# Two norm boundaries of a decoder step: one scale moved behind the contraction, and a third output chunk in the first feed-forward pass

## The reference

```python
for l in range(DEPTH):                       # DEPTH = 2
    hp, hs = rms_norm(xp, norm_mix_pre[l]), rms_norm(xs, norm_mix_pre[l])
    ...                                      # layer 0: retention and gated MLP; layer 1: sparse attention
    xp = xp + rms_norm(mp, norm_mix_post[l])
    xs = xs + rms_norm(ms, norm_mix_post[l])
    fp, cp = conv_ffn(rms_norm(xp, norm_ffn_pre[l]), zeros, f_w_in[l], ...)
    ...
    xp = xp + rms_norm(fp, norm_ffn_post[l])
    xs = xs + rms_norm(fs, norm_ffn_post[l])
```

## Time and profile before

| | us |
|---|---|
| median of 3 runs | 1612.62 (1607.88 to 1613.97) |
| profiled execution, whole | 1613.73 |
| its span in the profile | 1612.0 |
| PE busy | 1567.7 |
| DVE busy | 836.5 |
| ACT busy | 690.7 |
| POOL busy | 229.9 |

### The profile page before, as it was taken

The page is one execution under the profiler, slowest core; times in us unless marked ns, Lnnn a source line. Parts: engine busy times, 40 slices in busy tenths (PEclk is TensorE's granted clock), DMA queues, the critical chain, the costliest instruction groups (busy, mean ns, idle before and its releaser), DMA issues.

```text
span 1612.0 us, 29956 instructions
## 1 busy us (share of the span) xinstructions
PE 1567.7 (97%) x12323; PEld 1401.0 (87%) x12323; DVE 836.5 (52%) x1359; ACT 690.7 (43%) x1311; POOL 229.9 (14%) x574
## 2 busy tenths in 40 slices
PE   8999999999999999998999999999989999999998
PEld 7799989699999999996677566667989999999997
DVE  4855452655532555568234676743585552355523
ACT  5222134555532545432323565655545552355522
POOL 3000001300000000002013444422020000000001
PEclk9999999999999999999999899999999999999999
DMA  7322337023233332322344400033203324233231
GB/s 229 101 81 81 100 80 188 17 83 101 62 95 96 86 97 62 95 70 80 114 132 92 150 9 2 1 119 78 79 27 92 90 60 116 79 96 87 63 86 56
DMA packets 180274, 138.38 MB, mean 86 GB/s; under 512 B 11408, under 2 KB 164272, under 8 KB 180112
## 3 DMA queue, kind: packets, MB, share of 16 engines
q1 hardware_dynamic: 172288, 113.26, 24.4%
q0 software_dynamic: 7888, 23.79, 5.1%
HBM read 128.21 MB, written 13.01 MB: 88 GB/s over the span
## 4 chain that ended last, share of the span: by engine, by line
PE 89%; DVE 6%; ACT 2%; issue 1%; POOL 1%; DMA 0%; POOLq 0%; ACTq 0%; DVEq 0%
PE gemm L1150 42%; PE gemm L714 18%; PE gemm L725 9%; PE misc L683 6%; PE gemm L1290 3%; PE misc L1321 2%; PE misc L888 1%; DVE hL L1909 1%; PE misc L1426 1%; PE gemm L888 1%; PE misc L761 1%; DVE y L1983 1%; DVE y L1969 1%; PE misc L844 1%; PE misc L1315 0%
## 5 line engine op out<-in xcount | busy, mean ns | idle before, releaser
L1898 DVE TENSOR_TENSOR wL<-raw,wH 128x2048 fp32r<-128x2048 f32 (+1 forms) x106 | 219.6, 2072 | 151.0 <-ACT wH L1460 150.8
L1150 PE MATMUL gemm<-hH,wH 128*128 128x272 f32 x1280 | 268.5, 291 | 0.2
L1150 PE MATMUL gemm<-hH,wL 128*128 128x272 f32 x1280 | 264.8, 288 | 0.0
L1150 PE MATMUL gemm<-hL,wH 128*128 128x272 f32 x1280 | 264.0, 288 | 0.0
L1460 ACT ACTIVATE wH<-raw 128x2048 fp32r<-128x2048 f32 (+2 forms) x110 | 185.9, 1690 | 74.0 <-PE gemm L725 37.5
L1150 PEld LDWEIGHTS gemm<-hH,wH 128*128 128x128 f32 x1280 | 200.6, 188 | 6.1 <-issue 4.1
L1150 PEld LDWEIGHTS gemm<-hL,wH 128*128 128x128 f32 x1280 | 201.1, 188 | 0.0
L1150 PEld LDWEIGHTS gemm<-hH,wL 128*128 128x128 f32 x1280 | 199.9, 189 | 0.0
L2262 DVE SCALAR_TENSOR_TENSOR conv<-up,rows_t,conv 128x560 f32<-128x560 f32 x88 | 70.6, 802 | 208.2 <-ACT conv L1460 208.2
L1460 ACT ACTIVATE up<-gemm 128x32 f32<-128x32 f32 (+2 forms) x264 | 66.0, 324 | 175.0 <-PE gemm L1150 153.7
L714 PE MATMUL gemm<-hH,wH 128*128 128x272 f32 (+1 forms) x624 | 132.6, 294 | 0.9 <-issue 0.6
(11 more groups left out here) (416 smaller groups left out, 2725.5 us busy)
## 6 DMA issues: line engine op xcount, KB each, us to landing
raw<-in_f_w_in SPq DMA_DIRECT2D x88, 512.0 KB, 4.9
raw<-in_f_w_out SPq DMA_DIRECT2D x32, 704.0 KB, 4.6
raw<-in_e_w_in SPq DMA_DIRECT2D x12, 1024.0 KB, 5.1
raw<-in_o_w_in SPq DMA_DIRECT2D x10, 1024.0 KB, 5.1
raw<-in_e_w_out SPq DMA_DIRECT2D x4, 1024.0 KB, 6.1
raw<-in_o_w_out SPq DMA_DIRECT2D x16, 256.0 KB, 6.7
pages<-in_cache_cmp POOLq DMA_DIRECT2D x10, 256.0 KB, 4.1
xin<-in_x_prompt SPq DMA_DIRECT2D x4, 512.0 KB, 6.5
```

The costliest lines, as they stand in the source:

```text
L1150: ins = pe.matmul(gemm[odd][:, n, 0:TH], w, x[:, k, n * TH:(n + 1) * TH], start=(k == 0 and part == 0), stop=(k == nk - 1 and part == 2))
L1898: order(dve.tensor_tensor(unit_view(wL, u), unit_view(raw, u), unit_view(wH, u).bitcast(F32), ALU.subtract), lo_ready)
```

## The change

Six edits, four at place A and behind it, three at place B (POOL's is common to both).

1. Place A (`plain_norm`, `fill_plain`): h is x times the gain only; norm 4's scale is left out of it. For each tile DVE scales y straight from RS, adds x + y at once, and makes `hL` by one operation out of x, the gain and `hH`; ACT makes `hH` with the gain as its scale. The total stands behind tile 1, its root on ACT behind `hH` of tile 2, and the split of O_IN+1 with the reciprocal behind tile 4.
2. Norm 4's scale is spread by PE inside O_IN+1, ahead of the last tile's products, kept as a row by ACT, turned into a column of tokens by PE (`turn_rstd`), and kept again by ACT (`keep_rstd`). The copies out of PSUM of all token units then multiply by it; the sample rows get one more DVE operation a unit; the gates' sigmoid moves behind their turn, in five operations. The split of O_IN+2 stands ahead of this on ACT, and ahead of the sample rows on DVE.
3. POOL adds no tile at norms 3 and 5 (`POOLED_POSTS` keeps it at the first and last norm); DVE adds all eight.
4. Place B (`expanded_norms`): scaling y, adding, scaling x of one tile follow each other on DVE, the second and third waiting for the one ahead; `hL` is one tile behind. The split of F1+1 stands behind tile 2's step.
5. `first_three` in place of `first_pair`: from tile 3 on, PE also makes c2, the first chunk of F1+1, in banks b4 and b7; tiles 0 to 3 of it are made at tile 3, then one at each tile.
6. Units F1+1 and F1+2 are written out ahead of the loop (`peeled`), since F1+1 has only c3 left; idle products: 16 behind A's spread; 8 and 16 behind B's two spreads (before 10 and 10 at each place).

```diff
+            def third_products(k):
+                at = k * 256
+                wh, wl = wH[:, (F1 + 1) % 2, at:at + P], wL[:, (F1 + 1) % 2, at:at + P]
+                for part, (w, x) in enumerate(((wh, hH), (wh, hL), (wl, hH))):
+                    for z in range(2):
+                        ins = pe.matmul(misc[:, 3 * z, 0:TH], w, x[:, k, z * TH:(z + 1) * TH],
+                                        start=(k == 0 and part == 0), stop=(k == DC - 1 and part == 2))
+                return ins
-            def first_pair(u, fill):
+            def first_three(u, fill):
...
                         if k == DC - 1:
                             order(ins, gemm_done)
+                    if k == 3:
+                        unit(u + 1)
+                        for earlier in range(3):
+                            third_products(earlier)
+                    if k >= 3:
+                        ins = third_products(k)
+                order(ins, gemm_done)
...
+            def turn_rstd():
+                pe.wait_ge(squared, EXPANDED[3].spread_kept())
+                for t in range(NT):
+                    w = NS if t == 0 else P
+                    ins = pe.matmul(b7[0:w, t:t + 1], rstd_row[0:1, tile_start(t):tile_start(t) + w], ident[0:1, 0:1], start=True, stop=True)
+                order(ins, summed)
...
                 if u == O_IN + 1:
                     for k in ks:
                         pe.wait_ge(h_ready, DC * 3 + k + 1)
+                        if k == DC - 1:
+                            spread_rstd(4)
                         for t in range(1, NT):
                             ins = token_products(u, k, t)
                             if k == DC - 1:
                                 order(ins, gemm_done)
+                                if t == 2:
+                                    turn_rstd()
...
+                    for i in peeled:
+                        unit(u0 + i)
+                        for j in range(2):
+                            if (i, j) == (1, 0):
+                                continue
+                            c = c0 + 2 * i + j
+                            if j:
+                                pe.wait_ge(tail_set, e0 + i)
+                                pe.wait_ge(tail_ev, e0 + i)
+                            ffn_product((u0 + i) % 2, (c // 2, c % 2), j, DC, hH, hL)
...
+            def fill_plain(n, fill):
+                g = NORM_GAIN[n + 1]
+                for k in range(DC):
+                    act.wait_ge(x_ready, updated(n // 2, k))
+                    if k == 0:
+                        act.wait_ge(gemm_done, FIRST_CHUNK[FILL_AFTER[fill]])
+                    activate(hH[:, k, :], xT[:, k, :], ACT.Copy, h_hi, scale=gains[:, k, g:g + 1])
+                    if k == 2:
+                        total_root(n)
+            def keep_rstd(n):
+                act.wait_ge(rstd_ready, n + 1)
+                act.wait_ge(rows_stored, 128)
+                activate(halves(rstd_row[:, :]), RS, ACT.Copy, squared)
+                act.wait_ge(summed, EXPANDED[n].sums_done() + 1)
+                activate(rstd_col[0:NS, 0:1], b7[0:NS, 0:1], ACT.Copy)
+                activate(rstd_col[:, 1:NT], b7[:, 1:NT], ACT.Copy, squared)
+                order.wait()
...
+            def update(n, k, spread_out, row):
+                order(dve.scalar_tensor_tensor(row(y[:, k, :]), row(y[:, k, :]), gains[:, k, NORM_GAIN[n]:NORM_GAIN[n] + 1],
+                                               spread_out, ALU.mult, ALU.mult), y_scaled)
+                dve.wait_ge(y_scaled, DC * (n // 2) + k + 1)
+                order(dve.tensor_tensor(xT[:, k, :], xT[:, k, :], y[:, k, :], ALU.add), x_ready)
+            def plain_norm(n, fill, xs, next_split):
...
+                for k in range(DC + 1):
+                    if k < DC:
+                        update(n, k, RS, halves)
+                    if k == 1:
+                        total_square(n)
+                    if k:
+                        dve.wait_ge(h_hi, DC * fill + k)
+                        order(dve.scalar_tensor_tensor(hL[:, k - 1, :], xT[:, k - 1, :], gains[:, k - 1, g:g + 1], hH[:, k - 1, :].bitcast(F32),
+                                                       ALU.mult, ALU.subtract), h_ready)
+                    if k in (3, 7):
+                        dve.wait_ge(x_ready, updated(n // 2, k))
+                        order(dve.tensor_tensor(xs[:, k - 3:k + 1, :], xT[:, k - 3:k + 1, 0:NS],
+                                                gains[:, k - 3:k + 1, g:g + 1].to_broadcast([P, 4, NS]), ALU.mult), xs_ready)
+                    if k == 4:
+                        split_lo(next_split)
+                        dve.wait_ge(root_ready, n + 1)
+                        order(dve.reciprocal(rr[:, :], rq[:, :]), rec_ready)
+            def expanded_norms(n, fill):
...
+                for k in range(DC + 1):
                     if k < DC:
+                        update(n, k, ex.acc_x, lambda ap: ap)
+                        if k == 0:
+                            dve.wait_ge(rstd_ready, n + 1)
+                        dve.wait_ge(x_ready, updated(n // 2, k))
+                        order(dve.scalar_tensor_tensor(halves(y[:, k, :]), halves(xT[:, k, :]), gains[:, k, NORM_GAIN[n + 1]:NORM_GAIN[n + 1] + 1],
+                                                       RS, ALU.mult, ALU.mult), ht_ready)
+                    if k:
+                        fill_lo(fill, k - 1, y[:, k - 1, :])
                     if k == 2:
+                        split_lo(F1 + 1)
...
-            residual(1)
             pool.wait_ge(rows_stored, 128)
```

More of the change, by code:

```diff
@@ L264, in squared @@
             def squared(self, m, of_y):
[L265 removed]
+                return SQUARES_AFTER + 18 * self.turn + 2 * m + (2 if of_y else 1)
             def added(self, m, of_y):
@@ L379, in build_program, with updated, chunk_banks @@
         POOLED = (1, 3, 5)
+        POOLED_POSTS = (0, 3)
+        def updated(post, m):
+            before = sum(DC - (len(POOLED) if p in POOLED_POSTS else 0) for p in range(post))
+            return before + m + 1 - (sum(k < m for k in POOLED) if post in POOLED_POSTS else 0)
         def chunk_added(eng, post, m):
-            if m in POOLED:
-                eng.wait_ge(x_pooled, POOLED_AFTER + len(POOLED) * post + POOLED.index(m) + 1)
-            else:
-                eng.wait_ge(x_ready, (DC - len(POOLED)) * post + m + 1 - sum(k < m for k in POOLED))
+            if post in POOLED_POSTS and m in POOLED:
+                eng.wait_ge(x_pooled, POOLED_AFTER + len(POOLED) * POOLED_POSTS.index(post) + POOLED.index(m) + 1)
+            else:
+                eng.wait_ge(x_ready, updated(post, m))
+        THIRD = FIRST_CHUNK[F1] + 2
+        def chunk_banks(c):
+            return misc[:, 0:4:3, :] if c == THIRD else gemm[c % 2]
         def token_bank(u, t):
@@ L1657, in project_out @@
                 if first == O_OUT:
-                    expanded_roots(n)
+                    root(n)
+                    total_root(n)
+                    activate(halves(EXPANDED[n].acc_x), RS, ACT.Copy, squared)
                     return
@@ L1744, in _ @@
             split_hi(O_IN + 1)
-            norm_fill(2, 3)
+            fill_plain(3, 3)
+            split_hi(O_IN + 2)
+            keep_rstd(3)
             meet(act, order, 2)
@@ L1764, in _ @@
                     c = FIRST_CHUNK[u]
-                    activate(halves(gT[:, :]), chunk_ready(c)[0:48, :, 0:TH], ACT.Sigmoid, evacuated[c % 2])
+                    activate(halves(gT[:, :]), chunk_ready(c)[0:48, :, 0:TH], ACT.Copy, evacuated[c % 2])
                     act.wait_ge(g_turned, 1)
-                    activate(gN[:, :, :], b5[:, 0:48 * NT].rearrange("p (t e) -> p t e", t=NT), ACT.Copy, g_ready)
+                    for t in range(NT):
+                        w = NS if t == 0 else P
+                        activate(gN[0:w, t, :], b5[0:w, 48 * t:48 * t + 48], ACT.Sigmoid, g_ready if t == NT - 1 else None, scale=rstd_col[0:w, t:t + 1])
                     continue
@@ L1944, in add_gy, with total_square @@
                 order(dve.tensor_tensor(ex.acc_gy, ex.acc_gy, ex.tmp, ALU.add), added)
-            def expanded_norms(n, fill, xs=None, next_split=None):
+            def total_square(n):
                 ex, total = EXPANDED[n], EXPANDED[n].xy[:, 0:TQ]
-                dve.wait_ge(root_ready, n)
-                order(dve.reciprocal(rr[:, :], rq[:, :]), rec_ready)
-                dve.wait_ge(summed, SUMS_AFTER + ex.turn + 1)
+                dve.wait_ge(summed, ex.sums_done())
                 order.wait()
@@ L2297, in _ @@
             ffn(0)
-            expanded_norms(3, 3, xsO, O_IN + 1)
+            plain_norm(3, 3, xsO, O_IN + 1)
             meet(dve, order, 2)
```

94 lines of the change are left out of this document (47 added, 47 removed).

## The result

The changed kernel takes 1619.34 us (median of 10 runs, 1614.35 to 1625.20) against 1612.55 (1607.88 to 1613.97); the ratio is 1.0047, 95% interval [1.0033, 1.0060], so 5 to 10 us more, where +4.4 and 1617.0 were forecast. The profiled execution took 1614.66 (span 1613.0) and is the second shortest of the ten. It shows the mechanism of the forecast; why the median lies 4.7 above it was looked for by experiment, and is shown in part only. The granted clock on record for each execution points to the clock: 0.994 in the two shortest, 0.986 to 0.991 in the other eight.

The account below looks back on a forecast made before the run. PE was taken to hold 89% of the chain, with DVE setting its long holes. A -2.2 and B +6.6 gave +4.4 on the profiled 1613.73, so 1618.1, or 1617 for the median; range 1608.5 to 1622.5.

Parts of the forecast that it names:

- The rival on dearer waits: Places A and B: a DVE self-wait costs 0.3 beyond the duration, not 0.03, giving 1622; chance 0.1.
- its last rival: Place A gains in full: spread and turn hide, or DVE gains more without POOL; 1614.5; chance 0.06.
- the 1603 there: Time if A gains in full and "The first pass pays" holds with c0 early, as being 0.5% faster takes.
- its hole: Place B: PE stands about 4 us ahead of c4, until the split of F1+2 ends.
- the fall behind it: Place B: the clock falls behind the hole ahead of c4, +1.7, with 0 as the other end.
- the clock stays up: Place B: rival that the clock does not fall at c4, giving 1615.3; chance 0.2.
- The fall in the hole ahead of tile 2: Place B: clock fall in a 3.5 us hole, mostly on matmuls that wait anyway; +0.3, at most 1.7.
- The first pass pays: Place B: c4 starts when c3 ends, +0.8, not held by the split of F1+2; 1611.5; chance 0.2.
- the spread: Place A: PE's spread of norm 4's scale, now in its row rather than in the hole; +1.0.
- the turn: Place A: five small fp32 products on PE, now in its row rather than in the hole; +0.8.
- the wait for the column: Place A: ACT empties token tile 1 only after two small copies of the scale's column; +0.1, ends 0 and 0.6.
- At A the fall ahead of O_IN+1 was there before, and stays: Place A: the clock fall ahead of O_IN+1 is the same before and after; no term in the sum.

Follow-up runs that it names:

- b_alone: Changed kernel with place A taken back to before, with all that applies norm 4's scale later; 1619.56 us, ratio 1.0052 against before.
- split_first: Changed kernel, but ACT splits F1+2's weights and copies c2 out before gelu and aH of the first pair; 1615.86 us, ratio 1.0023 against before.
- a_idle_0: As a_alone, without the 16 idle products behind A's spread; 1609.22 us, ratio 0.9978 against before.
- a_idle_25: As a_alone, with 25 idle products in place of 16 behind A's spread; 1612.61 us, ratio 1.0001 against before.
- a_alone: Changed kernel with place B taken back to before, with the old expanded_norms and loop of units; 1613.96 us, ratio 1.0003 against before.
- c4_hole_filled: Changed kernel with 28 idle products in the hole ahead of c4, which made c4 2.5 late; 1621.73 us, ratio 1.0070 against before.
- c4_hole_filled_14: Changed kernel with 14 idle products in the hole ahead of c4; 1621.10 us, ratio 1.0046 against before, six runs.

## Why the prediction was right, and where it was off

**Bound and prices.** Right. A self-waiting scaling and add start 0.81 and 0.76 apart (forecast 0.80 and 0.74), `hL` of tile 3 ends 16.15 behind the first scaling (15.97). The rival on dearer waits falls with these rows. Two slips of the forecast change nothing: its 2.15 us hole is the second of its rows, not the third, and -4.1 for A in place of -2.2 gives 1615.1 where its last rival has 1614.5; for the 1603 there its terms do not suffice.

**B.** Right in mechanism and nearly in size: c4 +4.66 (forecast +4.6), its hole 3.46 (about 4), the fall behind it 1.56 (+1.7, with its rival "the clock stays up" wrong in this trace and in `b_alone`'s). The fall in the hole ahead of tile 2 (+0.3) was absent here, 0.5 in `split_first`, 1.2 in `b_alone`. By runs B alone costs 8.4 (6.0 to 10.8), for +6.6. "The first pass pays" fails: ACT did not get through sooner (from c0's copy to c2's 6.79, forecast 6.9). The forecast had c3 wait for POOL's rows, at +0.8 for c4 in that rival; `split_first`, where no other hole covers it, shows 1.4.

**A.** The terms of its work are right one by one: PE starts 4.15 earlier (4.2), the sample products -4.26 (-4.1), the spread takes 0.84 (+1.0), the turn 1.13 (+0.8), the wait for the column 0.2 (+0.1). Together they cost PE more than the 2.2 of these steps, since it loses about 0.1 more at each change to such work and back. The sample products of O_IN+2 show it, in the changed kernel and before:

```profile
763.17 1.06 PE L781 MATMUL misc<-raw,xsO 128*32 128x512 f32 x8
```

```profile
768.08 1.06 PE L761 MATMUL misc<-raw,xsO 128*32 128x512 f32 x8
```

They come 20.54 behind those of O_IN+1, 19.41 before, where the fall took some 1.6 of it (eight starts 0.40 to 0.57 apart, for 0.23 at the full clock). So the new work costs 2.7, and the terms sum to -1.6, inside the forecast's -3.2 to -1.0. The step that failed is "At A the fall ahead of O_IN+1 was there before, and stays". It does not stay as it was: it is gone or longer. Distances from the first spread, over the traces with the hole left open, are

| kernel | sample products | landmark | clock behind the sample products | clock 780 to 800 |
|---|---|---|---|---|
| before, `b_alone` | 27.20, 27.22 | 69.73, 69.71 | 0.74, 0.88 (750 to 756) | 1.00 |
| changed, `split_first`, `a_idle_0`, `a_idle_25` | 22.94 to 22.96 | 66.74 to 66.81 | 1.00 | 1.00 |
| `a_alone`, `c4_hole_filled`, `c4_hole_filled_14` | 22.95 | 69.41 to 69.64 | 0.50, 0.64, 0.50 (744 to 750) | 0.91 |

So A gives 3.0 (1.6 of it from before's fall) or, with the fall behind the landmark, costs 1.2; by runs of `a_alone` +0.5 (-1.6 to 2.6), and not -2.2. That is the term that was mis-sized. That the changed kernel's other executions went mostly the costly way would put them 4.2 above the profiled one, at 1618.9, and the median of these nine is 1619.83; none of them was traced, and five lie between 1619.83 and 1625.20, so A's two ways cannot be all of it. This is argued from `a_alone`'s groups and the three traces. What decides the way of one execution stays open. The Trainium skill (TensorE: Matmul & The Clock Gate, "What's actually happening") says that the point at which the clock changes varies from run to run of one kernel, as the chip's check does not start with the program; the two ways of one code in the table agree with that.

The forecast time lay 2.3 below the measured median. The forecast's sum, +4.4, would be +7.1 with A at +0.5 in place of -2.2; measured are +6.8.

## What to carry to other kernels

Work that PE did earlier was worth nothing here while the next unit's weights were still made behind the old order: move the split with it, and check on every engine what the next start waits for. A hole between two stretches of matmuls is to be priced with the clock behind it, over several executions, since one trace shows only one outcome; fill it by moving real work (here the sample products, worth 5.5 to 6.7 for a hole of 2.2) rather than by idle products.

## What the runs showed of the hardware

One code at A had two outcomes, 4.2 to 4.4 us apart in the traces. Keeping PE busier ahead of a hole did not help: judged by the groups of times (not by traces, and other stretches vary as much), the long stretch at 1.2 GHz came in eight of twelve runs with 16 idle products, in six of twelve with 25, and in none of ten without them. At B the start of F1's products 2.8 later (42 idle products) changed nothing, though the clock stayed up there (1.00 from 1178 to 1184, 0.72 before): c0's copy stayed 23.54 behind the first scaling.
